# Scan's norm and output projection as one stage, by channel tiles instead of token tiles

## The reference, cut to what matters

```
y = y_f + fl(y_b) + lp['d_skip'][:, None] * xs
y = rmsnorm(y.reshape(bsz, t, SSD_D_INNER) * jax.nn.silu(z), lp['ssd_norm_w'])
y_a = y @ lp['w_ssd_out']
...
merged = jax.nn.sigmoid(g_a) * y_a + jax.nn.sigmoid(g_b) * y_b2
return merged @ lp['w_o'], s_f, s_b, k, v
```

## Time and profile before

| | |
|---|---|
| median of 3 runs | 2992.23 us |
| the profiled execution, its time | 2992.27 us |
| its span, first to last instruction | 2990.5 us |
| mean granted clock of PE | 0.940 of full speed |
| norm stage, first instruction to the next stage's first | 1238.61 to 1271.08 us |
| projection stage, up to the next stage's first | 1271.08 to 1398.04 us |
| PE / DVE / ACT busy from 1238.6 to 1303.5 us | 45.10 / 28.21 / 18.39 us |

### The profile page before, as it was taken

One profiled execution on the slowest core, in us unless ns is written; L12 is line 12 of the kernel. 1 busy time (PEld: TensorE's weight loads), 2 busy tenths in 40 slices (PEclk: granted clock), 3 DMA queues, 4 the chain that ended last, 5 costly groups with the idle time before them and its releaser, 6 DMA issues. The chain is left out here.

```text
span 2990.5 us, 40641 instructions
## 1 busy us (share of the span) xinstructions
PE 2616.5 (87%) x15117; PEld 2278.1 (76%) x15117; DVE 2220.2 (74%) x3790; ACT 1047.3 (35%) x1515; POOL 713.5 (24%) x584
## 2 busy tenths in 40 slices
PE   4979999998899999598795248799999999999997
PEld 3967776777777777398695238789999998889896
DVE  2556666663277777623459999599999999999998
ACT  3223444443234333212323148233333333333332
POOL 0000000000266666100000038232323232432321
PEclk7989999999899999799897669899999999999998
DMA  6431111112322321342210015999999999999996
GB/s 243 171 118 47 46 61 69 56 61 87 124 90 89 106 89 58 119 176 106 93 56 30 27 57 225 376 409 407 398 403 397 400 399 409 381 404 402 401 400 245
DMA packets 147467, 615.36 MB, mean 206 GB/s; under 512 B 13168, under 2 KB 72336, under 8 KB 84496
## 3 DMA queue, kind: packets, MB, share of 16 engines
q1 hardware_dynamic: 110192, 345.26, 30.8%
q0 software_dynamic: 36864, 268.45, 21.9%
q10 hardware_dynamic: 288, 0.03, 0.0%
HBM read 557.29 MB, written 56.41 MB: 205 GB/s over the span
## 5 line engine op out<-in xcount | busy, mean ns | idle before, releaser
L2090 POOL DMA_INDIRECT p_uv<-in_uv_rows,merged x256 | 334.1, 1305 | 730.4 <-DVE merged L2253 656.2
L2110 PE MATMUL p_pa<-h2D,w_hi 128*128 128x384 f32 x1024 | 345.5, 337 | 7.3 <-DVE w_lo L2217 5.0
L2112 PE MATMUL p_pa<-h2D,w_lo 128*128 128x384 f32 x1024 | 344.8, 337 | 0.0
L2111 PE MATMUL p_pa<-h2D,w_hi 128*128 128x384 f32 x1024 | 344.7, 337 | 0.0
L2147 ACT ACTIVATE w_hi<-w_raw 128x2048 fp32r<-128x2048 f32 x126 | 241.5, 1917 | 282.9 <-PE p_py L2126 234.0
L2253 DVE SCALAR_TENSOR_TENSOR merged<-p_uv,p_sw,merged 128x1024 f32<-128x1024 f32 x256 | 331.0, 1293 | 9.2
L2239 DVE CUSTOM_DVE_ANT_0 p_uv<-p_uv,merged 128x1024 f32<-128x1024 f32 x256 | 310.1, 1231 | 16.8 <-DMA p_uv<-in_uv_rows,merged 16.8
L2124 PE MATMUL p_py<-w_hi,p_wh 128*128 128x512 f32 x768 | 304.5, 396 | 10.6 <-DVE w_lo L2217 10.6
L2217 DVE TENSOR_TENSOR w_lo<-w_raw,w_hi 128x2048 fp32r<-128x2048 f32 x126 | 288.8, 2292 | 30.9 <-ACT w_hi L2147 30.9
L105 DVE TENSOR_TENSOR w_lo<-w_raw,w_hi 128x2048 fp32r<-128x2048 f32 x64 | 155.8, 2436 | 209.8 <-ACT w_hi L100 209.5
L2125 PE MATMUL p_py<-w_lo,p_wh 128*128 128x512 f32 x768 | 304.1, 396 | 0.0
(11 more groups left out here) (357 smaller groups left out, 6063.1 us busy)
## 6 DMA issues: line engine op xcount, KB each, us to landing
w_raw<-in_w_stream SPq DMA_DIRECT2D x190, 1024.0 KB, 7.6
g_dram<-e_st SPq DMA_DIRECT2D x6, 4096.0 KB, 11.3
p_g<-g_dram SPq DMA_DIRECT2D x64, 384.0 KB, 17.2
t_ada<-in_w_ada SPq DMA_DIRECT2D x16, 1024.0 KB, 10.2
xc_dram<-c_xc SPq DMA_DIRECT2D x8, 1284.0 KB, 4.5
s_xx<-xc_dram SPq DMA_DIRECT2D x8, 642.0 KB, 6.0
s_bc<-xc_dram SPq DMA_DIRECT2D x8, 642.0 KB, 7.5
gate_dram<-s_gst SPq DMA_DIRECT2D x16, 320.0 KB, 5.4
```

The lines of the kernel that those rows point to most:

```text
L2090: nc.gpsimd.indirect_dma_start(uv[:, k % RING, :], None, K.uv_rows, bass.IndirectOffsetOnAxis(K.sidx[:, t, c:c + 1], 0)).then_inc(K.gather ...
L2110: nc.tensor.matmul(ps_a[m][:, :], wh[:, k, cols], K.h2D[0][:, k, :], start=k == 0, stop=False)
L2111: nc.tensor.matmul(ps_a[m][:, :], wh[:, k, cols], K.h2D[1][:, k, :], start=False, stop=False)
L2112: mm = nc.tensor.matmul(ps_a[m][:, :], wl[:, k, cols], K.h2D[0][:, k, :], start=False, stop=k == KD - 1)
```

## The change

The two stages become one, `phase_ssd_out`. It works by channel tiles:

- SP loads y by group of 256 channels for all tokens: eight loads of 640 KB in pieces of 1 KB (before: five of 1 MB in pieces of 8 KB), three buffers. The norm weights come as a [128, 16] column table of 8 KB instead of a copy for all partitions.
- For channel tile k PE does five transposes (three into one bank, two into the next); ACT writes the rounded part with the channel's norm weight as scale, DVE writes the rest with the same weight in one instruction. Sizes are 384 and 256 columns.
- The first quarter's matmuls are interleaved: the twelve matmuls of tile kk, then the transposes of tile kk + 2. The banks of the second set serve the transposes meanwhile. Quarters 1 to 3 run as before, but written out instead of in a loop of two rounds.
- The token factors are no longer applied to y. ACT writes five diagonal tiles (into the buffer `o_mb1`), PE multiplies them by a tile of ones, which gives the factors as a row on all partitions; ACT copies them to `rrow`. In each quarter POOL multiplies the gate (after its sigmoid) by that row, and DVE's product of gate and result waits for it.
- The hi step of weight unit 2 stands behind channel tile 12 on ACT, its lo step behind tile 14 on DVE.

```diff
+            rows(0)
+            sp.dma_start(wc[:, :], K.ssd_norm_w).then_inc(w_in, 16)
+            rows(1)
+            rows(2)
+            S.load(sp, U_SO + 3, 1)
+            for g in range(3, GROUPS):
+                rows(g)
+            block_dmas(0, 0)
+            sp.wait_ge(row_mm, 1)
+            block_dmas(1, 1)
...
+            def token_factors():
+                pe.wait_ge(diag_done, NT)
+                for t in range(NT):
+                    for h in range(2):
+                        a, b = max(t * P, h * TH), min((t + 1) * P, (h + 1) * TH)
+                        if a < b:
+                            mm = nc.tensor.matmul(ps[1][2 + h][:, a - h * TH:b - h * TH], K.ones[:, :], diag[:, t, a - t * P:b - t * P],
+                                                  start=True, stop=True)
+                mm.then_inc(row_mm, 1)
+
+            def transposes(k):
+                g = k // 2
+                pe.wait_ge(y_in[g % 3], 16 * (g // 3 + 1))
+                if k >= 2:
+                    pe.wait_ge(lo_done, 2 * (k - 1))
+                if k == 1:
+                    pe.wait_ge(row_done, 2)
+                for b in range(2):
+                    for t in range(HALF[b].start, HALF[b].stop):
+                        at = (t - HALF[b].start) * P
+                        mm = nc.tensor.transpose(tr_bank(k, b)[:, at:at + P], y[g % 3][:, t, (k % 2) * P:(k % 2 + 1) * P], K.ident[:, :])
+                    mm.then_inc(tr_done, 1)
...
+            transposes(0)
+            token_factors()
+            transposes(1)
+            for kk in range(NK):
+                half = kk // KD
+                if kk % KD == 0:
+                    S.ready(pe, U_SO + half)
+                pe.wait_ge(lo_done, 2 * kk + 2)
+                for m in range(2):
+                    mm = product(kk, 0, m, *weights(half))
+                if kk == NK - 1:
+                    mm.then_inc(mm_done, 1)
+                if kk % KD == KD - 1:
+                    pe.drain().then_inc(K.hilo_free, 1)
+                if kk + 2 < NK:
+                    transposes(kk + 2)
...
+        def _(pool):
+            pool.wait_ge(row_done, 2)
+            for c in range(4):
+                pool.wait_ge(sig_done, 2 * c + 2)
+                nc.gpsimd.tensor_tensor(ga[c % 2][:, :, :], ga[c % 2][:, :, :], rrow[:, :].unsqueeze(1).to_broadcast([P, 2, T]),
+                                        ALU.mult).then_inc(scaled, 1)
...
+            def high(k):
+                for b in range(2):
+                    act.wait_ge(tr_done, 2 * k + b + 1)
+                    nc.scalar.activation(K.yT[0][:, k, columns(b)], tr_bank(k, b)[:, 0:width(b)], ACT.Copy, scale=wc[:, k:k + 1]).then_inc(hi_done, 1)
...
+            def low(k):
+                for b in range(2):
+                    dve.wait_ge(hi_done, 2 * k + b + 1)
+                    nc.vector.scalar_tensor_tensor(K.yT[1][:, k, columns(b)], tr_bank(k, b)[:, 0:width(b)], wc[:, k:k + 1],
+                                                   K.yT[0][:, k, columns(b)].bitcast(F32), ALU.mult, ALU.subtract).then_inc(lo_done, 1)
...
                 dve.wait_ge(mm_done, c + 1)
-                dve.wait_ge(sig_done, 2 * c + 2)
+                dve.wait_ge(scaled, c + 1)
...
-            for phase in (phase_ssd_norm, phase_ssd_out):
-                run_phase(nc, K, phase)
+            run_phase(nc, K, phase_ssd_out)
```

More of the change, by code:

```diff
@@ L1384, in _ @@
                     S.lo(dve, U_ZG + u + 2, u % 2)
[L1389 to L1451, removed]
@@ L1459, in phase_ssd_out @@
     sb = lambda n, s, d=F32: ctx.enter_context(nc.sbuf_tensor(n, s, d))
+    GW = HPG * HP
+    NK = DI // P
     ga = [sb(f"o_ga{i}", [P, 2, T]) for i in range(2)]
@@ L1469, in _, with rows @@
         def _(sp):
+            def rows(g):
+                if g >= 3:
+                    sp.wait_ge(tr_done, 4 * (g - 2))
+                sp.dma_start(y[g % 3][:, :, :], K.y_dram[:, g * GW:(g + 1) * GW].rearrange("(t p) c -> p t c", p=P)).then_inc(y_in[g % 3], 16)
             def block_dmas(c, s):
@@ new lines, in product, with weights @@
+            def product(kk, s, m, wh, wl):
+                k, cols = kk % KD, slice(m * P, (m + 1) * P)
+                for lhs, rhs, f, l in ((wh, K.yT[0], kk == 0, False), (wh, K.yT[1], False, False), (wl, K.yT[0], False, kk == NK - 1)):
+                    for h in range(2):
+                        mm = nc.tensor.matmul(ps[s][2 * m + h][:, 0:TH], lhs[:, k, cols], rhs[:, kk, h * TH:(h + 1) * TH], start=f, stop=l)
+                return mm
+            def weights(half):
+                return [x[half][:, :].rearrange("p (k c) -> p k c", k=KD) for x in (K.whi, K.wlo)]
@@ new lines, in _ @@
+            for c in range(1, 4):
+                pe.wait_ge(K.so_free, 4 * c + 4)
+                for half in range(2):
+                    S.ready(pe, 2 * c + (U_SO + half))
+                    for m in range(2):
+                        for k in range(KD):
+                            mm = product(half * KD + k, c % 2, m, *weights(half))
+                    if half:
+                        mm.then_inc(mm_done, 1)
+                    pe.drain().then_inc(K.hilo_free, 1)
+        @block.gpsimd
@@ L1512, in _ @@
+        def _(pool):
[4 more added lines that the diff above has]
+                                        ALU.mult).then_inc(scaled, 1)
         @block.scalar
         def _(act):
+            def high(k):
+                for b in range(2):
+                    act.wait_ge(tr_done, 2 * k + b + 1)
+                    nc.scalar.activation(K.yT[0][:, k, columns(b)], tr_bank(k, b)[:, 0:width(b)], ACT.Copy, scale=wc[:, k:k + 1]).then_inc(hi_done, 1)
+            act.wait_ge(ms_done, 1)
+            nc.scalar.activation(ss[:, :], ss[:, :], ACT.Sqrt).then_inc(rt_done, 1)
+            act.wait_ge(r_done, 1)
+            for t in range(NT):
+                nc.scalar.activation(diag[:, t, :], K.ident[:, :], ACT.Copy, scale=ss[:, t:t + 1]).then_inc(diag_done, 1)
+            act.wait_ge(w_in, 16)
+            high(0)
+            act.wait_ge(row_mm, 1)
+            for h in range(2):
+                nc.scalar.activation(rrow[:, h * TH:(h + 1) * TH], ps[1][2 + h][:, 0:TH], ACT.Copy).then_inc(row_done, 1)
+            for k in range(1, NK):
+                high(k)
+                if k == 12:
+                    S.hi(act, U_SO + 2, 0)
```

52 lines of the change are left out of this document (33 added, 19 removed).

## The result

The changed kernel takes 2977.29 us (median of 5 runs, 2975.61 to 2978.4) against 2994.01 us (5 runs, 2986.39 to 2996.74): a ratio of 0.9947 with a 95% interval of 0.9936 to 0.9958. The forecast was 2978.2, counted down from the 2992.23 us of the first three runs before the change. The profiled execution took 2977.66 us, with a span of 2975.9 at a mean granted clock of 0.939.

A forecast was written before the change was run, and what follows sets the result against it. The stage was taken as serial: y loaded, normed, transposed, split, then PE's product. Terms 1248.7 + 28.1 + 8.4 + 0.9 + 2.0 + 0.8 = 1288.9, 14.6 us less; minus 0.5 gives 14.1, so 2978.2 us, range 2974 to 2983.

The forecast's parts named there:

- Until the first product: Stage head: y lands at 1242.8, then transposes, factor matmuls and copies take 5.9 us; first product at 1248.7 against 1271.66.
- Rival 3: Stage head: first group of y lands after 8.5 us instead of 4.2, 4.3 us more, 2982.5; chance 0.07.
- A tile at 2.36 us, nothing binds: Interleaved quarter: PE needs 2.36 us a tile; ACT, DVE and the 2.39 us latency stay hidden, under 0.6 us in hand.
- rival 1: Interleaved quarter: the relay binds, latency reaches 4.0 us and a tile 2.9, 7 us more, 2985; chance 0.12.
- The wait before tile 15: End of the interleaved quarter: PE waits 0.9 us because DVE does a weight unit behind tile 14.
- The lower clock, 2.0 us: Start of the interleaved quarter: products at PE's lower clock level lose between nothing and 2.5 us, taken as 2.0.
- Rival 2: Mixed quarter: the clock stays down, quarter 1 starts at 1316.6, 13.1 us later than before, time 3005.9; chance 0.04.
- Quarter 1 at 50.3 us: First matmul of quarter 1 at 1288.9 against 1303.54, 14.6 us less.
- DVE's wait for POOL costs nothing: Behind quarter 0: POOL's gate product takes 3.0 us, and DVE still finishes weight unit 3 with 3 us in hand.
- The end, 0.5 us: Stage end: POOL clears 21 semaphores instead of 6 at about 0.03 us each, 0.5 us more.
- Quarters 1 to 3 the same: Later quarters: PE does the same work, written out instead of looped; no change in time was counted.
- Rival 5: Later stages: the gain is given back if the last stage's own length varies that much, 2990; chance 0.04.

The follow-up runs named there:

- distance one: Changed kernel with the transposes of tile kk + 1, instead of kk + 2, behind the product of tile kk; 3001.17 us, ratio 1.003 to the kernel before.
- half lo: Changed kernel with the lo step of weight unit 2 split into halves behind tiles 13 and 14; 2979.15 us in one run.
- warm: Changed kernel plus eleven small matmuls on PE while y is in flight; 2974.83 us, ratio 0.9945 to the kernel before.
- POOL four times: Changed kernel with POOL doing its product of gate and token factors four times in each quarter; 2986.20 us, ratio 0.9978 to the kernel before.
- serial: Changed kernel with all transposes and splits before all products, in one stage; 2991.28 us, ratio 0.9995 to the kernel before.
- combined: Changed kernel plus eight early matmuls, token factors before transposes, and unit 2's lo step in halves; 2974.22 and 2973.89 us, ratios 0.9933 and 0.9944 to before.

## Why the prediction was right, step by step

The forecast of 2978.2 us was met within 1 us, and by the mechanism that it named. That it was so close is luck: single executions of one kernel spread over several microseconds, the stage became 15.4 and 15.2 us shorter where 14.1 were forecast, and by the five runs on each side the time fell 16.7 us, by those on one chip 15.0. By its own steps:

- *Until the first product* (10.1 us after the stage's start): 10.6. Data came after 4.8 us instead of 4.2, the factors' matmuls took 2.8 instead of 2.4; ACT's copies and the second group took 0.4 less together. Rival 3, a late start, did not happen: pieces of 1 KB land in a median of 4.5 us for 640 KB.
- *A tile at 2.36 us, nothing binds*: 2.31. ACT's 0.59 and 0.48 were 0.58 and 0.47, DVE's 0.62 and 0.48 were 0.62 and 0.48. The latency of 2.39, which rival 1 put in doubt, is 2.21 by distance one. In the changed kernel itself DVE is done with a tile at 1254.92, 2.15 us after its transposes (1252.77), and the product that needs it starts at 1255.54: about the 0.6 us in hand that I had named. So rival 1 did not happen.
- *The wait before tile 15*: 0.8 us from start to start (a bracket of 0.54) instead of 0.9, with the place and the cause as said, shown by half lo. The 2.13 us after which I had DVE free do not follow from my rows: DVE ends tile 14 after 2.34 us of latency (2.39 less the last crossing), its group began 2.36 us before tile 15's, and the weight unit takes 2.29. That is 2.27, and a wait of 1.0.
- *The lower clock, 2.0 us*: mis-sized. From the first product to the second are 3.62 us (1247.31 to 1250.93) instead of 2.31, and after that all tiles are at full pace: 1.3 us, the same as the 38.90 - 37.60 us by which warm is shorter. The first part of the head at the lower clock, 1.7 us by warm, lay in the terms before. The two drains cost 0.8 together, as said. The rises before the change, by rows 4, were nearer 1253.6 and 1277.4 than my 1253.3 and 1277.2. Rival 2 did not happen: granted 1.00 from 1252 to the end of the quarter. The Trainium skill, "TensorE: Matmul & The Clock Gate", section "Part 4: PE-mode transpose", would have transposes not count as busy for the clock. The interleaved quarter doesn't test that: transposes are a quarter of each tile, and distance one kept 1.00 with 1.50 us of each 4.08 idle. What disagrees is the trace of the kernel before, where the clock rose (0.72 over 1253 to 1254) when PE had done nothing but transposes since 1248.33.
- *Quarter 1 at 50.3 us* (1288.9): 49.5. The head was 0.5 longer, the tiles 0.6 and the lower clock 0.7 shorter.
- *DVE's wait for POOL costs nothing*: so it is, by 5.7 us of cover, more than the 3 that I gave. POOL took 3.03 us in quarter 0, the value I had taken, and 4.15 in the later quarters, above my upper bound of 3.8; beside other work it cost nothing.
- *The end, 0.5 us*: mis-sized. It is 1.1 us (2.37 against 1.23), 0.07 to 0.08 a semaphore instead of 0.03. I had read the slope from two stages, 12 and 6 semaphores, whose ends differ by more than clearing, and even these give 0.13 / 6 = 0.02.
- *Quarters 1 to 3 the same*: they are 1.1 us shorter to DVE's last work (92.20 against 93.27). PE's bracket of 0.75 us in the middle, at the loop's second round, is gone and each quarter takes 29.00, where quarters 1 and 2 took 29.66 and 29.26. Not foreseen; it just covers the term before.
- *Rival 5, the gain given back*: not seen. The rest of the span spreads over 1592.5 to 1595.4 us before and 1592.1 to 1595.1 after, and the time fell by as much as the stage.

What I hadn't priced is what hangs on that margin. The distance of two tiles is worth 23 us, more than the whole change.

## What to carry to other kernels

Where a preparation goes over several engines and the product over one, price both the busy time and the latency of a tile, and give the product's engine as much other work as the latency lasts: two tiles of distance made a latency of 2.2 us vanish, one tile made the change a loss. Price a wait from start to start of the work around it, since the idle bracket showed 0.54 us of a wait that cost 0.8. Per-row factors that commute with the product can be applied where an engine is idle, and the transfers and instructions for them then leave the head of the stage. Measure such a change on the stage's own length, which repeated within 0.7 us in the three kernels profiled twice, while the whole varied by 3 to 5 for reasons outside it.

## What the runs showed of the hardware

- PE held the upper clock with waits of 1.50 us in every 4.08 (distance one, 2.50 of 4.00 us busy at 1.00), while a single wait of 3.46 us was followed by the lower one (POOL four times, 0.61 and 0.82). The length of a wait alone does not tell: in serial, 1.44 us before 1262.07, behind waits of 0.2 to 0.7, was followed by 0.75 and 0.64, and 1.66 us before the first product (1268.24) by 0.50 from 1270 to 1272. The rise came at a different delay after PE's first work in each kernel: granted 0.58 over 1236 to 1240 in the combined kernel, which began at 1236.32 (about 3 us), 0.70 over 1242 to 1244 in the warm one, which began at 1237.54 (under 6), and 0.94 over 1250 to 1252 in the changed one, which began at 1241.52 and stood still for 0.95 us on the way (under 9; 8.0 in its second profile, so one kernel varies too).
- POOL's product of 1280 columns is 3.03 us in quarter 0, where DVE waits, and 4.15 us in the later ones, where DVE's product of `o_mb` and `o_gb` (1304.81, 1.49 us) begins just before it (1304.96). In the POOL experiment POOL began first (1304.99), and the same DVE product took 4.23 us instead of 1.49. It ended at 1310.32, 1.35 us after POOL's product, which itself had begun while DVE's lo step ran (to 1306.18) and took 3.98 us instead of 2.95. So each of the two that starts second is stretched by about as long as the other still runs, and that can be DVE:

```profile
1306.09 4.23 DVE L1585 TENSOR_TENSOR o_mb<-o_mb,o_gb 128x1280 f32<-128x1280 f32 x1
```

- Clearing a semaphore at a stage's end costs 0.07 us (30 more, 2.07 us longer). By that the 44 of the scan stage are some 3 us, an estimate; no run has fewer there.
